# A mixture-of-experts stage: the overflow of the fullest expert computed beside its own block instead of in a 33rd block

## The chip, the cores and the metric

The kernel runs on one core of a Trainium2 chip. The metric is the device time of one execution in microseconds. A profiled execution shows each engine: PE is TensorE, DVE VectorE, ACT ScalarE, POOL GpSimd, SP the queue that issues the loads of weights.

## The reference

Two transformer blocks on 512 tokens of width 1024. The first has a gated linear attention mixer and then the expert layer that this change is about; the second block (retention, a state space mixer, differential attention, two dense feed-forward layers) follows and is not touched. The expert layer is:

```python
logits = (xt @ w_router + b_router)            # 512 tokens, 32 experts
top_vals, top_idx = lax.top_k(logits, 4)
weights = jax.nn.softmax(top_vals, axis=-1)
# per expert e, over its tokens:
gate, up = jnp.split(xblk @ w_gu[e] + b_gu[e], 2, axis=-1)
gate = jnp.minimum(gate, 7.0); up = jnp.clip(up, -7.0, 7.0)
act = (up + 1.0) * gate * jax.nn.sigmoid(1.702 * gate)
y[token] += weight * (act @ w_down[e] + b_down[e])
```

There are 2048 pairs of a token and an expert. Each expert has 3 x 1024 x 1024 weights in fp32, 12.6 MB, and the 32 of them are read once each. For the inputs of this case expert 10 has 131 tokens, expert 17 124, expert 8 121, and expert 0 has 56.

## The kernel before, in words

All engines run one program each, written out in order, and wait for one another by semaphores. The expert stage is `moe_pe`, `moe_act`, `moe_dve` and `moe_pool` (from L2418), with SP in `program_sp`.

Routing (`route_dve`, L2038) ranks the experts by their number of tokens, expert 0 always first. Ranks 0 to 15 take the even positions 0, 2, ... 30 and get wide blocks of 128 rows; ranks 16 to 31 take the odd positions and get narrow blocks of 64 rows. What an expert has beyond its block (`CAP`, 128 or 64) goes to overflow blocks of 128 rows. The first overflow block is block 32, part of the straight program (`N_BLK = 33`); further ones are run by a loop behind the stage (`looped`, L2596) with its own weight loads, whose number of turns is counted on the chip. Block 32 is always run, whether there is an overflow or not.

Each block has 24 weight pieces of 128 x 1024 fp32 (512 KB): 8 of the gate half, 8 of the up half, 8 of the down matrix. The order of the pieces is gate(e), down(e-1), up(e), so phases of 8 wide and of 8 narrow pieces alternate on every engine. SP issues the loads one after another (`fetch`, L438) into 26 slots in turn; a load waits until PE has used the piece that was in the slot.

Wide blocks use every piece three times as fp32r: ACT rounds it (`conv_hi`, L464, out to one of four small buffers), DVE subtracts to get the rest (`conv_lo`, L472, over the raw piece in its slot), and PE makes 6 matmuls of 512 columns (`rows_pe`, L2269): high x high, low x high, high x low, two halves each. Narrow blocks use the raw piece in fp32 (`half_rows_pe`, L2347): the 64 rows are held as weights twice, the two halves of the outputs go to the two halves of the array at once. Each fp32 matmul shows as two instructions in the trace, so a narrow piece has 4.

The rows of a block are gathered by POOL from `hm_scratch`, turned on PE (`turn_pe` for wide, `narrow_xturn_pe` for narrow), multiplied, passed through the gate on ACT and DVE, turned again, multiplied by the down pieces, scaled by the routing weight on ACT and added to `sum_scratch` by a POOL DMA that accumulates (`block_sum`, L2531). Each sum waits for the sum before it. When all sums have landed (`rows_stored`) the loop, if it has turns, and then `combine_sp` (L2698) with the read of `sum_scratch` follow. The first ten pieces of the next layer's weights are loaded on the same SP queue behind the last expert pieces.

The matmul and turn instructions are recorded in helpers: L272 is every matmul, L288 every transpose, L192, L199, L203 and L207 are VectorE operations, L237 ScalarE activations, L451 the loads of SP.

Of the kernel before, what the change touches and what calls it, by code (L numbers as in the profile page):

```python
# [334 lines left out]
def build(nc, ins, out):  # L335
# [35 lines left out]
    s_g = [sem("s_gather0"), sem("s_gather1")]  # L371
    s_y = [sem("s_ystore0"), sem("s_ystore1")]
# [158 lines left out]
    ids, P_FIRST = {}, {}  # L531
    R_MOE = len(W.raws)
# [30 lines left out]
    plan_down(32)  # L563
# [1455 lines left out]
    LH, RH, RP = r(12288, 2048, 128), r(11392, 768, 48), a(4096, 768, 48)  # L2019
# [11 lines left out]
    WSL, ROWF = a(K0 + 208, 48), a(K0 + 304, 48)  # L2031
    ROWI = a(K0 + 256, 48).bitcast(I32)
# [3 lines left out]
    RQ, RTMP = r(5120, 2304, 144), a(K0 + 400, 48)  # L2036

    def route_dve(v):  # L2038
# [35 lines left out]
        v.stt(POS, SMALL, 1.0 - 2.0 * NWIDE, POS, ALU.mult, ALU.add)  # L2074
        v.tt(BASE, CNT, CAP, ALU.subtract)
# [5 lines left out]
        v.stt(BASE, BASE, 32.0, POS, ALU.add, ALU.subtract)  # L2081
# [12 lines left out]
        v.tt(BLK, T1, pos, ALU.add)  # L2094
        OH4 = OH.rearrange("p (t k e) -> p t k e", k=4, e=32)
# [5 lines left out]
        for h in range(2):  # L2101
            is_ = slice(8 * h, 8 * h + 8)
            v.tt(LH[:, is_, :], iota.unsqueeze(1).to_broadcast([128, 8, 128]),
                 OF4[:, is_].unsqueeze(2).to_broadcast([128, 8, 128]), ALU.is_equal)
            v.tt(RP[:, is_, :], iota[:, 0:48].unsqueeze(1).to_broadcast([128, 8, 48]),
                 BK4[:, is_].unsqueeze(2).to_broadcast([128, 8, 48]), ALU.is_equal)
# [17 lines left out]
        v.ts(XI[:, 31:32], XI[:, 31:32], 1.0, 0.0, ALU.subtract, ALU.max)  # L2124
# [13 lines left out]
        v.copy(RQ[:, :, 0:48], RP)  # L2138
        v.tt(RQ[:, :, 48:96], RP, WTH.bitcast(F32).unsqueeze(2).to_broadcast([128, 16, 48]), ALU.mult)
        v.tt(RQ[:, :, 96:144], RP, WTL.unsqueeze(2).to_broadcast([128, 16, 48]), ALU.mult, "slot parts")  # L2140

    def slot_weights_pe(p):

        b = p.bank("slot weights", at=6)
        p.wait_ge(*dve("slot parts"))
        p.claim("slot weights")
        for i in range(16):
            p.mm(PB[b][:, 0:144], LH[:, i, :], RQ[:, i, :], i == 0, i == 15, "slot weights" if i == 15 else None)

    def slot_weights_dve(v):  # L2150

        v.wait_ge(*pe("slot weights"))
        b = bank_of("slot weights")
        v.copy(WSL, b[:, 48:96])
        v.tt(WSL, b[:, 96:144], WSL, ALU.add)
        v.copy(ROWF[:, 0:NBLK], IDXI)
        v.ts(RTMP, b[:, 0:48], SPARE[:, 1:2], SPARE[:, 0:1], ALU.mult, ALU.add)
# [10 lines left out]
    def slot_halves_pe(p):  # L2168

        b = p.bank("slot halves", at=7)  # L2170
        p.wait_ge(*dve("halves"))
        p.claim("slot halves")
        p.mm(PB[b][:, 0:16], TWICE, narrow(WSL), True, True)
        p.mm(PB[b][:, 16:32], TWICE, narrow(ROWF), False, True, "slot halves")

    def slot_halves_dve(v):

        v.wait_ge(*pe("slot halves"))
        b = bank_of("slot halves")
# [11 lines left out]
    def route_pe(p):  # L2191
        rows_out_pe(p, 0)
        b = p.bank("ranks")
        p.wait_ge(*dve("sel"))
        p.claim("ranks")
        sel_ = a(o + 240, 128)
        p.mm(PB[b][:, 0:128], tri, sel_, True, True)
        p.mm(PB[b][:, 128:256], ones, sel_, False, True, "ranks")
        for t in range(1, 4):
            rows_out_pe(p, t)  # L2200
        b = p.bank("slots")
        for i in range(16):
            p.wait_ge(*dve("slots", i // 4))
            if i == 0:
                p.claim("slots")
            p.mm(PB[b][:, 0:48], LH[:, i, :], RH[:, i, :], i == 0, i == 15, "slots" if i == 15 else None)
# [5 lines left out]
    XTs, ATs = a(3072, 512, 64), a(3584, 512, 128)  # L2212
    UT, AC, ZT, GZ = a(6144, 1024), a(7168, 1024), a(8192, 1024), a(9216, 1024)
# [68 lines left out]
    def gu_pe(p, z, e, what, lhs, after=None):  # L2282
        name, b = ("gu", e, what), 2 + 2 * what
        open_pe(p, name, b, lhs, what * 1024)
        p.wait_ge(*z.dve("xg", e))
        for k in range(8):
            rows_pe(p, z, b, XTh[:, k, :], XTl[:, k, :], k, name)
            if after is not None:
                after(k)

    def down_pe(p, z, e, lhs):
        name = ("down", e)
        open_pe(p, name, 6, lhs, 2048)
# [33 lines left out]
    N_BLK = 33  # L2327
# [89 lines left out]

    def moe_pe(p):  # L2418
# [3 lines left out]
        for e in range(N_BLK):  # L2422
            def beside_gate(k):
                if e and k == 2 and is_wide(e):
                    narrow_aturn_pe(p, e - 1)
                if k == 4 and not is_wide(e):
                    aturn_pe(p, MOE, e - 1)
                if e == 0 and k == 2:
                    slot_weights_pe(p)

            def beside_up(k):
                if k == 3 and is_wide(e) and e + 1 < N_BLK:
                    narrow_xturn_pe(p, e + 1)
                if k == 3 and not is_wide(e):
# [13 lines left out]
        aturn_pe(p, MOE, N_BLK - 1)  # L2448
        down_pe(p, MOE, N_BLK - 1, sel(N_BLK - 1))
# [8 lines left out]
    def moe_act(q):  # L2458
        xturn_act(q, MOE, 0)
        for e in range(N_BLK):  # L2460
            if is_wide(e):
# [3 lines left out]
                gate_act(q, MOE, e)  # L2465
                four_units(q, conv_hi)
# [3 lines left out]
                if e + 1 < N_BLK:  # L2470
                    turned_copy_act(q, "xg", e + 1, 0, XTs)
            else:
                halves_act(q, MOE, ("at", e - 1), ATh)
                four_units(q, conv_hi)
# [5 lines left out]
                xturn_act(q, MOE, e + 1)  # L2480
                four_units(q, conv_hi)
        halves_act(q, MOE, ("at", N_BLK - 1), ATh)
        four_units(q, conv_hi)
        four_units(q, conv_hi)
        store_wide(q, N_BLK - 1)

    def moe_dve(v):
        xturn_dve(v, MOE, 0)
        for e in range(N_BLK):
            if is_wide(e):  # L2490
# [3 lines left out]
                gate_dve(v, MOE, e)  # L2494
                four_units(v, conv_lo)
# [3 lines left out]
                up_dve(v, MOE, e)  # L2499
            else:  # L2500
# [20 lines left out]
    def gather_narrow(g, idx, s_):  # L2521
        g.e.indirect_dma_start(out=XG[1][0:64, :], out_offset=None, in_=hm_d,
                               in_offset=bass.IndirectOffsetOnAxis(ap=idx, axis=0)).then_inc(s_, 16)

    def sum_narrow(g, idx, s_):

        g.e.indirect_dma_start(out=sum_d.rearrange("t (h c) -> (t h) c", h=2),
                               out_offset=bass.IndirectOffsetOnAxis(ap=idx, axis=0), in_=YB[1][:, 0:512],
                               in_offset=None, compute_op=ALU.add).then_inc(s_, 16)

    def block_sum(g, e):  # L2531
        g.wait_ge(*act("rows", e))
        if e:
            g.wait_ge(s_y[(e - 1) % 2], 16 * ((e - 1) // 2 + 1))
        if is_wide(e):
            sum_rows(g, 0, ROWI[:, e:e + 1], s_y[0])
        else:
            sum_narrow(g, ROWI[:, e:e + 1], s_y[1])

    def moe_pool(g):  # L2540
# [5 lines left out]
        for e in range(N_BLK):  # L2546
# [4 lines left out]
            else:  # L2551
                gather_narrow(g, IDXI[0:64, e:e + 1], s_g[1])
# [43 lines left out]
    def looped(q, name, body):  # L2596
# [6 lines left out]
        n_ = q.e.value_load(SI[0:1, 16:17], min_val=0, max_val=15)  # L2603
# [6 lines left out]
    def loop_sp(s):  # L2610
        def body(x):
            if at_pe.known:
                which[0] = x.e.value_load(SI[0:1, bass.ds(x.loop[0] + 1, 1)], min_val=0, max_val=31)
# [16 lines left out]
    def loop_dve(v):  # L2630
        def body(x):
            x.copy(WJ, WSL[:, bass.ds(x.loop[0] + 33, 1)])
            x.copy(SELJ[0:96, :], SELX[0:96, bass.ds(x.loop[0] + 1, 1)].to_broadcast([96, 128]), "sel")
# [1439 lines left out]
    def program_sp(s):  # L4073
        load_sp(s)
        for i in range(len(W.pieces)):
            if P_FIRST.get(i, 0) and at_pe.known:
                e = P_FIRST[i]
                s.wait_ge(*dve("ids"))
                ids[e] = s.e.value_load(SIP[0:1, e:e + 1] if e < 32 else SI[0:1, 0:1], min_val=0, max_val=31)
# [77 lines left out]
```

## Time and profile before

| what | value |
|---|---|
| median of 3 runs | 3135.3 us (3132.92 to 3135.72) |
| the profiled execution: time, span | 3138.64 us, 3136.4 us |
| PE busy over the span | 2866.5 us (91%) |
| DVE, ACT, POOL busy | 1645.6 us (52%), 1201.9 us (38%), 269.5 us (9%) |
| DMA moved | 634.58 MB, mean 202 GB/s |
| expert stage | from about 456 to about 1580 us of the span |

The span is what lies between the first and the last instruction of the trace; the time adds 2.2 us around it. All stretches below are microseconds from the span's start. A busy PE is not PE at its peak, and a share is an average over stages with different limits, so the rows further down are from inside the expert stage.

### The profile page before, as it was taken

The page shows a single profiled execution, that of the slowest core. Times are in us where ns is not written, and L with a number is a line of the kernel's source. Part 1 is how long each engine was busy: PE and PEld are TensorE (multiplying, and loading weights), DVE is VectorE, ACT ScalarE, POOL GpSimd, SP SyncE. Part 2 cuts the span into 40 slices and gives each one's busy share as a digit, 9 for nine tenths or more (in the row PEclk, how much of TensorE's full clock was granted, in tenths as well). Part 3 has the DMA queues.
Part 4 walks back from the last instruction along what each step waited for, and adds up shares of the span by engine and source line. Part 5 has one row for each costly group of instructions (what it writes and reads, how often), then busy time and mean ns, then how long its engine had stood idle before and what let it go on. Part 6 is the DMA issues. An engine that isn't in the chain of part 4 may idle for free.

```text
span 3136.4 us, 35266 instructions
## 1 busy us (share of the span) xinstructions
PE 2866.5 (91%) x13014; PEld 2047.2 (65%) x13014; DVE 1645.6 (52%) x2034; ACT 1201.9 (38%) x1549; POOL 269.5 (9%) x233
## 2 busy tenths in 40 slices
PE   6988879999999999999979778999998988999998
PEld 3856656655455555555567567888886755888887
DVE  5557556655555545555654535344356556543445
ACT  3242325544444544444532114322243256332334
POOL 1054721010010010000000000000000000000000
PEclk8998969999999999999979879999999988999999
DMA  7244739999999999999943022233332210223210
GB/s 223 73 137 166 269 140 383 397 391 396 397 392 394 396 394 393 395 393 392 368 159 95 13 108 74 91 98 98 97 101 74 81 35 20 89 90 106 88 61 27
DMA packets 224021, 634.58 MB, mean 202 GB/s; under 512 B 20038, under 2 KB 38484, under 8 KB 222980
## 3 DMA queue, kind: packets, MB, share of 16 engines
q1 hardware_dynamic: 207984, 577.70, 50.0%
q0 software_dynamic: 11760, 42.99, 4.9%
q10 hardware_dynamic: 4100, 11.59, 1.0%
q8 instruction: 104, 1.70, 0.2%
q14 instruction: 73, 0.60, 0.1%
HBM read 603.89 MB, written 28.31 MB: 202 GB/s over the span
## 4 chain that ended last, share of the span: by engine, by line
PE 63%; DMA 15%; DVE 9%; SPq 7%; ACT 3%; issue 2%; DVEq 0%; ACTq 0%; POOLq 0%
PE ps L272 61%; SPq L451 7%; DMA ring<-in_w_gu 7%; DMA arena<-in_w_gu 4%; DMA ring<-in_w_down 3%; DVE arena L192 2%; PE ps L288 2%; ACT arena L237 1%; ACT wunits L464 1%; DVE ring_r L472 1%; DVE arena L203 1%; DVE arena L211 1%; DVE arena L215 1%; DMA arena<-in_ctx 1%; DVE arena_r L203 1%
## 5 line engine op out<-in xcount | busy, mean ns | idle before, releaser
L272 PE MATMUL ps<-arena_r,wunits 128*128 128x512 f32 (+1 forms) x3552 | 1112.8, 395 | 15.6 <-DVE arena_r L192 7.8
L472 DVE TENSOR_TENSOR ring_r<-ring,wunits 128x1024 fp32r<-128x1024 f32 (+1 forms) x533 | 638.4, 1217 | 716.8 <-ACT wunits L464 709.8
L464 ACT ACTIVATE wunits<-ring 128x1024 fp32r<-128x1024 f32 (+1 forms) x533 | 552.4, 1050 | 835.6 <-PE ps L272 647.7
L272 PEld LDWEIGHTS ps<-arena_r,wunits 128*128 128x128 f32 x3552 | 672.1, 191 | 165.3 <-issue 15.8
L272 PE MATMUL ps<-arena_r,ring_r 128*128 128x512 f32 (+1 forms) x1776 | 696.0, 392 | 0.0
L272 PE MATMUL ps<-wunits,arena_r 128*128 128x512 f32 x1984 | 570.1, 401 | 57.5 <-ACT wunits L464 47.4
L272 PEld LDWEIGHTS ps<-wunits,arena_r 128*128 128x128 f32 x1984 | 369.0, 190 | 163.9 <-ACT wunits L464 35.7
L272 PEld LDWEIGHTS ps<-arena_r,ring_r 128*128 128x128 f32 x1776 | 338.0, 190 | 70.7
L272 PE MATMUL ps<-arena 128*64 128x512 f32 (+10 forms) x1566 | 307.8, 438 | 50.2 <-DVE arena L207 16.1
L272 PEld LDWEIGHTS ps<-arena 128*64 128x64 f32 (+5 forms) x1566 | 168.5, 181 | 172.4 <-issue 84.1
L272 PE MATMUL ps<-ring,arena 128*64 128x512 f32 (+1 forms) x1080 | 261.0, 601 | 10.2 <-issue 5.7
L272 PE MATMUL ps<-ring_r,arena_r 128*128 128x512 f32 x756 | 256.1, 401 | 8.6 <-DVE ring_r L472 5.0
L237 ACT ACTIVATE arena<-ps 128x512 f32<-128x512 f32 (+4 forms) x222 | 133.8, 603 | 210.2 <-PE ps L272 156.3
L272 PEld LDWEIGHTS ps<-ring_r,arena_r 128*128 128x128 f32 x756 | 139.7, 190 | 58.8 <-DVE ring_r L472 30.0
L272 PEld LDWEIGHTS ps<-ring,arena 128*64 128x64 f32 (+1 forms) x1080 | 75.8, 139 | 153.1 <-issue 108.2
L472 DVE TENSOR_TENSOR arena_r<-arena,wunits 128x1024 fp32r<-128x1024 f32 x118 | 141.6, 1223 | 51.3 <-ACT wunits L464 48.9
L288 PE MATMUL ps<-KC,arena 128*128 128x128 f32 (+3 forms) x742 | 110.1, 291 | 49.9 <-DVE arena L203 15.9
L464 ACT ACTIVATE wunits<-arena 128x1024 fp32r<-128x1024 f32 x118 | 123.5, 1058 | 76.8 <-DMA arena<-in_w_gu 59.3
L192 DVE TENSOR_TENSOR arena_r<-ps,arena_r 128x1024 fp32r<-128x1024 f32 (+1 forms) x38 | 44.4, 1169 | 200.7 <-ACT arena_r L237 200.2
L288 PEld LDWEIGHTS ps<-KC,arena 128*128 128x128 f32 (+3 forms) x742 | 86.5, 154 | 92.4 <-issue 49.4
L237 ACT ACTIVATE arena<-arena 128x512 f32<-128x512 f32 (+5 forms) x140 | 73.8, 527 | 139.4 <-DVE arena L192 85.2
L237 ACT ACTIVATE arena_r<-ps 128x1024 fp32r<-128x1024 f32 (+2 forms) x39 | 37.8, 970 | 232.6 <-PE ps L288 232.2
(176 smaller groups left out, 1970.8 us busy)
## 6 DMA issues: line engine op xcount, KB each, us to landing
ring<-in_w_gu SPq DMA_DIRECT2D x382, 512.0 KB, 15.9
ring<-in_w_down SPq DMA_DIRECT2D x170, 512.0 KB, 16.9
arena<-in_w_gu SPq DMA_DIRECT2D x146, 512.0 KB, 15.9
arena<-in_w_down SPq DMA_DIRECT2D x94, 512.0 KB, 16.4
ring<-in_w_ada SPq DMA_DIRECT2D x48, 512.0 KB, 5.4
ring<-in_ffn_w_gate SPq DMA_DIRECT2D x44, 512.0 KB, 3.7
ring<-in_ffn_w_up SPq DMA_DIRECT2D x44, 512.0 KB, 3.7
ring<-in_ffn_w_down SPq DMA_DIRECT2D x40, 512.0 KB, 3.6
```

The source lines that it names most:

```text
L192: self.inc(self.e.tensor_tensor(o, x, y, op), key)
L203: self.inc(self.e.scalar_tensor_tensor(out=o, in0=x, scalar=s, in1=y, op0=op0, op1=op1), key)
L211: self.inc(self.e.reciprocal(o, x), key)
L215: self.inc(self.e.tensor_reduce(o, x, AX.X, op), key)
L237: self.inc(self.e.activation(o, x, f, **kw), key)
L272: ins = self.e.matmul(o, l_, r_, start=start, stop=stop, skip_group_check=True)
L288: ins = self.e.transpose(o, x, self.ident[0:k, 0:k])
L451: s.e.dma_start(dst, w.src()).then_inc(w.sem, 16)
L464: q.inc(q.e.activation(h, raw, ACT.Copy), (st.tag, "hi", i))
L472: q.inc(q.e.tensor_tensor(lo, raw, h.bitcast(F32), ALU.subtract), (st.tag, "lo", i))
```

## The change

Block 32 is taken out (`N_BLK = 32`), with its 24 pieces, its gather and its sum. Position 20 (`TWIN`) now belongs to the fullest expert beside expert 0 (rank 1), which changes places with rank 10, and its cap is 192 rows: 128 in the wide block 20 and up to 64 in a twin block. The twin is computed in fp32 in two halves of the array, like a narrow block, from the raw pieces of block 20 while they lie in their slots. PE's order at block 20 is two twin pieces ahead, then one twin piece and one wide piece in turn, in all three phases (gate, up, down). DVE's `conv_lo` of these 24 pieces waits until PE has read the raw piece. The twin has a gather of its own (issued behind that of block 12), a turn beside block 19, gate, up and row scaling behind those of block 20 (the down phase of both lies in block 21), and a sum of its own behind the sum of block 20.

The stage now ends with block 31, a narrow one: its last phase is 8 narrow down pieces. Tables of 48 columns have 50. The loop behind the stage now starts at overflow block 0 instead of 1 and has no turn where nothing is left over. Its core:

```diff
-    for e_ in range(33):
+    for e_ in range(32):
...
+        v.ts(BASE, RANK, 1.0, 64.0, ALU.is_equal, ALU.mult)
+        v.tt(CAP, CAP, BASE, ALU.add)
+        v.stt(POS, BASE, (TWIN - 2) / 64.0, POS, ALU.mult, ALU.add)
+        v.ts(BASE, RANK, TWIN / 2.0, 2.0 - TWIN, ALU.is_equal, ALU.mult)
+        v.tt(POS, POS, BASE, ALU.add)
...
+        v.ts(T1f, OFf, 127.5, None, ALU.is_gt, None)
+        v.stt(OFf, T1f, -128.0, OFf, ALU.mult, ALU.add)
+        v.stt(BKf, T1f, 32.0 - TWIN, BKf, ALU.mult, ALU.add)
...
     def conv_lo(q, st, i):
...
+            if st.tag == "w" and U_TWIN <= i < U_TWIN + 24:
+                q.wait_ge(*pe("twin read", i))
...
     def gu_pe(p, z, e, what, lhs, after=None):
...
+        if e == TWIN:
+            open_halves_pe(p, ("twin", what), 7, twin_sel(), what * 1024)
+            p.wait_ge(*act("twin xt"))
+            for k in range(2):
+                twin_rows_pe(p, 7, TWX[:, k, :], what, k)
         p.wait_ge(*z.dve("xg", e))
         for k in range(8):
+            if e == TWIN and k + 2 < 8:
+                twin_rows_pe(p, 7, TWX[:, k + 2, :], what, k + 2)
             rows_pe(p, z, b, XTh[:, k, :], XTl[:, k, :], k, name)
...
     def down_pe(p, z, e, lhs):
...
+        if e == TWIN:
+            open_halves_pe(p, ("twin", 2), 5, twin_sel(), 2048)
+            p.wait_ge(*act("twin at"))
...
+    def twin_rows_pe(p, b, lhs, part, k):
+
+        i = U_TWIN + 8 * part + k
+        u = W.units[i]
+        land(p, u.w)
+        _, raw, _ = unit_tiles(u)
+        for h, o_, cs in each_half(b):
+            p.mm(o_, lhs, raw[:, cs], False, k == 7, ("twin", part) if k == 7 and h else None, h == 1)
+        p.note(("twin read", i))
...
+    def twin_gate_act(q):
+        q.wait_ge(*pe("twin", 0))
+        q.act(TWZ, PB[7], ACT.Sigmoid, "twin gate", scale=1.702)
...
+    def twin_up_dve(v):
+        v.wait_ge(*pe("twin", 1))
+        v.ts(UT[:, 0:512], PB[7], -6.0, 8.0, ALU.max, ALU.min)
+        v.free(("twin", 1))
+        v.stt(TWA, TWG, TOP, UT[:, 0:512], ALU.min, ALU.mult, "twin acts")
...
     def moe_pe(p):
...
+                if k == 1 and e == TWIN - 1:
+                    twin_xturn_pe(p)
...
+                if k == 7 and e == TWIN + 1:
+                    twin_aturn_pe(p)
...
-        aturn_pe(p, MOE, N_BLK - 1)
-        down_pe(p, MOE, N_BLK - 1, sel(N_BLK - 1))
+        narrow_aturn_pe(p, N_BLK - 1)
+        narrow_down_pe(p, N_BLK - 1)
...
     def block_sum(g, e):
...
+        if e == TWIN:
+            g.wait_ge(*act("twin rows"))
+            g.wait_ge(s_y[0], 16 * (e // 2 + 1))
+            sum_narrow(g, TWY, ROWI[:, 32:33], s_yt)
```

## Rows read from the trace of the kernel before

**Rows 1.** The page: busy tenths of the DMA engines in 40 slices.
```profile
DMA  7244739999999999999943022233332210223210
```

**Rows 2.** Windows: stretch, length, busy time of each engine, clock, DMA share, GB/s.
```profile
471.00:491.00 20.00, 18.14 (x89) 11.83 (x89) 13.36 (x14) 9.18 (x10) 2.92 (x1) 1.00 0.98 359
...
740.51:1424.58 684.07, 634.48 (x2802) 358.18 (x2802) 369.50 (x320) 316.85 (x320) 58.60 (x40) 0.99 1.03 394
```

**Rows 3.** The chain of waits, expert stage: start, length, what.
```profile
570.51 1.04 PE ps L288 x8
...
631.61 1.04 PE ps L288 x8
...
740.51 1.02 PE ps L288 x8
...
1424.58 1.02 PE ps L288 x8
```

**Rows 4.** Timeline, routing and the stage's start: start, length, engine, line.
```profile
420.02 0.19 DVE L203 SCALAR_TENSOR_TENSOR arena<-arena 128x32 f32<-128x32 f32 x1
...
426.06 0.62 DVE L203 SCALAR_TENSOR_TENSOR arena<-arena 128x128 f32<-128x128 f32 x2
...
446.34 1.60 SPq L451 DMA_DIRECT2D ring<-in_w_gu  x2
...
455.78 2.08 PE L272 MATMUL ps<-wunits,arena_r 128*128 128x512 f32 x4 [7.45 <-DVE arena_r L192]
```

**Rows 5.** DMA queues and issues, 1000 to 1400 us: share; us to landing.
```profile
q1 hardware_dynamic: 40512, 147.51, 93.3%
q0 software_dynamic: 3072, 9.44, 9.3%
...
ring<-in_w_gu SPq DMA_DIRECT2D x122, 512.0 KB, 16.4
```

**Rows 6.** Timeline of PE, a narrow phase and part of a wide one.
```profile
1030.77 0.41 PE L272 MATMUL ps<-BPT,arena 96*64 96x512 bf16 x2
1031.01 3.60 PE L272 MATMUL ps<-ring,arena 128*64 128x512 f32 x16
1034.54 1.09 PE L288 MATMUL ps<-KC,arena 128*128 128x128 f32 x8
1035.56 3.65 PE L272 MATMUL ps<-ring,arena 128*64 128x512 f32 x16
...
1051.92 1.07 PE L272 MATMUL ps<-wunits,arena_r 128*128 128x512 f32 x4
...
1053.28 1.07 PE L272 MATMUL ps<-wunits,arena_r 128*128 128x512 f32 x4
```

**Rows 7.** Waits of SP's queue, 470 to 680 us: total, times, longest.
```profile
SPq L451 <- PE ps L272: 53.7, 67, 3.7
```

**Rows 8.** The page, costliest groups: busy and mean ns, idle before.
```profile
L472 DVE TENSOR_TENSOR ring_r<-ring,wunits 128x1024 fp32r<-128x1024 f32 (+1 forms) x533 | 638.4, 1217 | 716.8 <-ACT wunits L464 709.8
```

**Rows 9.** DMA issues, 1544.5 to 1545.5 us: us from issue to landing.
```profile
ring<-in_w_down SPq DMA_DIRECT2D x1, 512.0 KB, 16.7
```

**Rows 10.** The chain of waits at the stage's end.
```profile
1545.42 8.76 DMA sum_scratch<-arena
...
1573.22 5.96 DMA sum_scratch<-arena
```

**Rows 11.** Timeline at the stage's end, SP and PE.
```profile
1543.72 0.93 SPq L451 DMA_DIRECT2D ring<-in_w_down  x1
...
1584.98 3.68 PE L288 MATMUL ps<-KC,ring 128*128 128x128 f32 x16 [13.37 <-DMA ring<-sum_scratch]
```

**Rows 12.** Windows at the stage's end, columns as in rows 2.
```profile
1556.00:1560.00 4.00, 2.48 (x7) 1.31 (x6) 2.54 (x3) 3.59 (x4) 0.00 (x0) 0.50 0.72 252
```

**Rows 13.** The page: issues of w_gu, KB each, us to landing.
```profile
ring<-in_w_gu SPq DMA_DIRECT2D x382, 512.0 KB, 15.9
...
arena<-in_w_gu SPq DMA_DIRECT2D x146, 512.0 KB, 15.9
```

More of the change, by code:

```diff
@@ L531, in build @@
     ids, P_FIRST = {}, {}
+    U_TWIN = len(W.units) + 12 * TWIN
     R_MOE = len(W.raws)
@@ L2137, in route_dve @@
             v.wait_ge(s_, 32)
-        v.copy(RQ[:, :, 0:48], RP)
-        v.tt(RQ[:, :, 48:96], RP, WTH.bitcast(F32).unsqueeze(2).to_broadcast([128, 16, 48]), ALU.mult)
-        v.tt(RQ[:, :, 96:144], RP, WTL.unsqueeze(2).to_broadcast([128, 16, 48]), ALU.mult, "slot parts")
+        v.copy(RQ[:, :, 0:NBLK], RP)
+        v.tt(RQ[:, :, NBLK:2 * NBLK], RP, WTH.bitcast(F32).unsqueeze(2).to_broadcast([128, 16, NBLK]), ALU.mult)
+        v.tt(RQ[:, :, 2 * NBLK:3 * NBLK], RP, WTL.unsqueeze(2).to_broadcast([128, 16, NBLK]), ALU.mult, "slot parts")
     def slot_weights_pe(p):
@@ L2147, in slot_weights_pe @@
         for i in range(16):
-            p.mm(PB[b][:, 0:144], LH[:, i, :], RQ[:, i, :], i == 0, i == 15, "slot weights" if i == 15 else None)
+            p.mm(PB[b][:, 0:3 * NBLK], LH[:, i, :], RQ[:, i, :], i == 0, i == 15, "slot weights" if i == 15 else None)
     def slot_weights_dve(v):
@@ L2173, in slot_halves_pe @@
         p.mm(PB[b][:, 0:16], TWICE, narrow(WSL), True, True)
-        p.mm(PB[b][:, 16:32], TWICE, narrow(ROWF), False, True, "slot halves")
+        p.mm(PB[b][:, 16:32], TWICE, narrow(ROWF), False, True)
+        p.mm(PB[b][:, 32:33], TWICE, WSL[:, 32:33], False, True)
+        p.mm(PB[b][:, 33:34], TWICE, ROWF[:, 32:33], False, True, "slot halves")
     def slot_halves_dve(v):
@@ L2205, in route_pe @@
                 p.claim("slots")
-            p.mm(PB[b][:, 0:48], LH[:, i, :], RH[:, i, :], i == 0, i == 15, "slots" if i == 15 else None)
+            p.mm(PB[b][:, 0:NBLK], LH[:, i, :], RH[:, i, :], i == 0, i == 15, "slots" if i == 15 else None)
     XG = [a(0, 1024), a(1024, 1024)]
@@ L2293, in down_pe, with twin @@
         open_pe(p, name, 6, lhs, 2048)
+        def twin(k):
+            twin_rows_pe(p, 5, TWT[:, k % 4, k // 4 * 64:k // 4 * 64 + 64], 2, k)
+        if e == TWIN:
+            open_halves_pe(p, ("twin", 2), 5, twin_sel(), 2048)
+            p.wait_ge(*act("twin at"))
+            for k in range(2):
+                twin(k)
         p.wait_ge(*z.dve("at", e))
         for k in range(8):
+            if e == TWIN and k + 2 < 8:
+                twin(k + 2)
             rows_pe(p, z, 6, ATh[:, k, :], ATl[:, k, :], k, name)
@@ L2416, in narrow_rows_act, with twin_sel, twin_xturn_pe, twin_aturn_pe @@
         q.free(("down", e))
+    def twin_sel():
+        return SELB[0:96, TWIN:TWIN + 1].to_broadcast([96, 64])
+    def twin_xturn_pe(p):
+        name = ("twin xt",)
+        p.wait_ge(s_gt, 16)
+        p.bank(name, at=0)
+        p.claim(name)
+        for k in range(8):
+            p.tp(PB[0][:, k * 64:(k + 1) * 64], TWR[:, k * 128:(k + 1) * 128], name if k == 7 else None)
+    def twin_aturn_pe(p):
+        name = ("twin at",)
+        p.wait_ge(*dve("twin acts"))
+        p.bank(name, at=0)
+        p.claim(name)
+        for c in range(4):
+            p.tp(PB[0][:, c * 128:(c + 1) * 128], TWA[:, c * 128:(c + 1) * 128], name if c == 3 else None)
+    def twin_copy_act(q, name, o_):
+        q.wait_ge(*pe(name))
+        q.copy(flat(o_), PB[0], name)
+        q.free((name,))
+    def twin_rows_pe(p, b, lhs, part, k):
[9 more added lines that the diff above has]
+        q.act(TWZ, PB[7], ACT.Sigmoid, "twin gate", scale=1.702)
+    def twin_gate_dve(v):
+        v.wait_ge(*act("twin gate"))
+        v.stt(TWG, PB[7], 7.0, TWZ, ALU.min, ALU.mult)
+        v.free(("twin", 0))
+    def twin_up_dve(v):
[3 more added lines that the diff above has]
+        v.stt(TWA, TWG, TOP, UT[:, 0:512], ALU.min, ALU.mult, "twin acts")
+    def twin_rows_act(q):
+        q.wait_ge(*pe("twin", 2))
+        q.act(TWY, PB[5], ACT.Copy, "twin rows", scale=WSL[:, 32:33])
+        q.free(("twin", 2))
     def moe_pe(p):
@@ L2433, in beside_up @@
                     narrow_xturn_pe(p, e + 1)
-                if k == 3 and not is_wide(e):
+                if k == 3 and not is_wide(e) and e + 1 < N_BLK:
                     xturn_pe(p, MOE, e + 1, 0, gathered(e + 1))
@@ L2612, in body @@
             if at_pe.known:
-                which[0] = x.e.value_load(SI[0:1, bass.ds(x.loop[0] + 1, 1)], min_val=0, max_val=31)
+                which[0] = x.e.value_load(SI[0:1, bass.ds(x.loop[0], 1)], min_val=0, max_val=31)
             for i in range(len(LW.pieces)):
@@ L2632, in body @@
             x.copy(WJ, WSL[:, bass.ds(x.loop[0] + 33, 1)])
-            x.copy(SELJ[0:96, :], SELX[0:96, bass.ds(x.loop[0] + 1, 1)].to_broadcast([96, 128]), "sel")
+            x.copy(SELJ[0:96, :], SELX[0:96, bass.ds(x.loop[0], 1)].to_broadcast([96, 128]), "sel")
             for i in range(NUNIT):
@@ L4078, in program_sp @@
                 s.wait_ge(*dve("ids"))
-                ids[e] = s.e.value_load(SIP[0:1, e:e + 1] if e < 32 else SI[0:1, 0:1], min_val=0, max_val=31)
+                ids[e] = s.e.value_load(SIP[0:1, e:e + 1], min_val=0, max_val=31)
             fetch(s, W, i)
```

86 lines of the change are left out of this document (52 added, 34 removed).

## The prediction

> **What bounds the kernel now.** I read the page first, for where the span is dense, then the chain of waits from 380 to 1600 us, then windows, waits and the timeline inside that stretch, which is the expert stage. The slices of the page say that the DMA engines are full from slice 6 to slice 19 and nowhere else for long [rows 1]; there the reader is to see a stage of 1.1 ms that moves weights all the time. The windows give the stretch from 740.51 to 1424.58 us its numbers: DMA share 1.03, PE busy 634.48 of 684.07 us, clock 0.99 [rows 2]. Both are nearly full, so the question is which of them sets the pace. The chain answers it. The 8 transposes of a wide block start 61.1 us apart in the first part (570.51 to 631.61, full clock) and 68.4 us apart later ((1424.58 - 740.51) / 10) [rows 3]. A pair of blocks (one wide, one narrow) thus costs PE 61.1 us when it never waits, and 68.4 us when it waits for weights: PE starts at 455.78 us with full slots [rows 4], is late, catches up 7.3 us a pair, and from about 680 us on it is paced by landings.
>
> DMA's pair of 68.4 us has two parts. The hardware queue that carries the weights has 93.3 of 102.6 parts, the software queue of the gathers and sums 9.3 [rows 5]. So 48 weight pieces take 62.2 us, **1.296 us a piece**, and 6.2 us go to the gather and the sum of both blocks. A wide block gathers and adds twice the bytes of a narrow one (128 rows of 4 KB against 64), so these are 6 units of **1.03 us**.
>
> **What goes.** Block 32 is a wide one: 24 pieces x 1.296 = 31.1 us of transfers and one wide gather, 2.1 us. Its sum stood behind the last weights; in the new order the sum of block 31 stands there, and the twin's sum takes its place among the weights, so the count of sums before the last landing is unchanged. For the last landing: -33.2 us.
>
> **What the twin adds on the DMA side.** No weights (it multiplies the pieces of block 20 in place), one narrow gather: +1.0 us.
>
> **What the twin adds on PE.** A narrow piece is 4 fp32 instructions; 16 of them (4 pieces) take from 1031.01 to 1034.54, so 0.88 us a piece [rows 6]. 24 x 0.88 = 21.1. Three openings of two halves, 0.24 each (1030.77 to 1031.01) = 0.7. Eight transposes of the rows, at most the 1.02 of eight full ones (1034.54 to 1035.56), and four of the activations, 0.5: 1.5. Then the alternation, which no row shows: a piece of the twin now stands between wide rows, so the array goes from full width to two halves and back, 7 groups in each of 3 phases, 42 changes. Below: nothing (narrow phases run on into transposes in 3.53 us, 8 slots of 0.43 would be 3.44). Above: a whole wide matmul each, (1053.28 - 1051.92) / 6 = 0.227 us [rows 6], 9.5 us. I take 0.12, nearest to the 0.09 left over in the 3.53: 5 us. Sum 28 us, between 23 and 33.
>
> The Trainium skill speaks against such an alternation: TensorEngine Tiling (Array Packing), section Key Properties, says that a change of tiling mode drains the engine. With the warm constant of 0.166 us of TensorE: Matmul & The Clock Gate, section Single matmul latency, 42 drains would be an estimate of 7 us instead of 5; no row here shows such a drain in isolation.
>
> **Does PE's extra work reach the end?** Blocks 20 and 21 cost PE 61.1 + 28 = 89 us against 69.4 on the DMA side: PE is 20 us late after them, and 3 us more at its worst, since a last narrow phase gains that much back. Two rows say what a late PE does to DMA. In the steady part a piece lands 16.4 us after its issue [rows 5], that is 11.5 of the 26 slots at 68.4 / 48 = 1.425 us; the other 14.5 slots are 20.6 us of room before SP has to wait for a slot, and then 16.4 us of queue are to be emptied before an engine idles. The views agree: between 680 and 1500 us SP's waits have no entry at all, between 470 and 680, where PE is late by some 3.5 pairs x 7.3 = 26 us at first, SP waits 53.7 us in 67 pieces [rows 7], and the DMA share still is 0.98 there [rows 2]. So a lag of 23 us has been seen and cost DMA at most 5% of some 20 us: **+1.0 us**, bounds 0 and 8. It is worked off at 7.3 us a pair in 2.8 pairs; 5 pairs are left.
>
> The added waits: VectorE may write the low part over a raw piece only after the twin has read it. PE reads two pieces ahead; after the first twin piece it still has two twin pieces (1.76) and four wide matmuls (0.9) to do before it needs that low part, and the subtraction takes 1.22 us [rows 8]: covered. ScalarE's copy of the twin's turned activations holds back its conversions of the down pieces by some 3 us; PE fills this with two twin pieces, and what stays is lag, in the bounds above. The POOL queue waits for the landing of block 20's sum before it issues the twin's; behind it stands the gather for block 24, needed a pair later.
>
> **Routing.** Before the block ids exist VectorE gets 5 operations of 32 columns (0.19 + 0.02 us) and 3 of 128 columns (two take 0.62, so 0.31) [rows 4], and slightly wider compares, 0.1. SP issues the pieces of block 1 at 446.34, right behind the ids [rows 4], with DMA not yet full. So this is on the path: 1.05 + 0.93 + 0.1 = **+2.1 us** (bounds 1 and 4, as the gather chain runs beside it).
>
> **The end of the stage.** The last weight piece of before is issued at 1543.72 and takes 16.7 us [rows 9, 11]: landed at 1560.4. Behind it stand most of a wide phase on PE, the scaling and the sum, which is issued at 1573.22 and lands 5.96 later, 1579.18 [rows 10]: 18.8 us behind the last landing. PE resumes at 1584.98 [rows 11], another 5.8 us later. After: the last eight pieces are narrow. Their activations are ready before they land (8 x 1.3 = 10.4 us ahead, minus 0.9 for the last up piece and about 3 for clamp, product, turn and copy), so PE follows the landings and ends 1 us after the last. But PE idles there a few us, and in such a gap the granted clock went to 0.50 (1.2 GHz) in the same place of before [rows 12]; 8 pieces at half rate take 14 us instead of 7, of which I count 2 us. Scaling 0.7, issue 0.4, and the sum 8.8, as the narrow one issued at 1545.42 beside busy queues took 8.76 [rows 10] (5.96 is the lower bound). 1 + 2 + 0.7 + 0.4 + 8.8 = 12.9 against 18.8: **-5.9 us**, bounds -10 and 0. The ten pieces of the next layer are issued earlier and still land when the sums are read back: +1.0 (0 to 3).
>
> **Sum.** -31.1 - 2.1 + 1.0 + 1.0 + 2.1 - 5.9 + 1.0 = -34.0 us. What follows is PE at work without a wait for transfers, so it moves with it. The profiled execution took 3138.6 us (span 3136.4), the sum gives 3104.6 for it; it stands 3.3 above the median of the runs, 3135.3, which gives **3101.3 us**.
>
> **Rivals.** (1) The lag of PE reaches DMA. For it: the stage has only 7.3 us of PE slack a pair, the 28 us is one lump, and the changes of width are priced by no row. Against: the start of the stage [rows 2, 7]. If nothing of the lag were absorbed the 20 us come back: 3121 us; a part of it, 3113 to 3121. Chance 0.10. (2) The end gives more: the sum lands in 6 us, no half clock, free queues: 4 us below, and routing beside other work, 1: 3096. It is inside the range, chance 0.12. (3) Slower than before: the loop behind the blocks runs. It decides from one expert on that overflows its cap. Now one overflow has a block, and the page shows 528 pieces of w_gu, 33 x 16, so no turn was run [rows 13]; after it must be the fullest expert beside expert 0 and hold at most 192. A turn has nothing beside it: gather and sum at 8.8 each, two turns with their splits at about 3.3, three wide phases at 8 x 1.36 + 0.6, activations and scaling about 4, 63 us: 3164. Against it: the routing worked out from the inputs gives 131 rows to expert 10, 124 to the next, 56 to expert 0, and 61 to the seventeenth in the order, which is the first with 64 places. Chance 0.03.
>
> **How the numbers follow.** The forecast case has 0.75: 3101. The bounds of its terms, added as if independent, are about 9 us to either side; down to 3090 holds rival 2, up to 3114 takes in the milder half of rival 1. A change under 0.2% (6 us) is what a measurement of this kernel can't tell from none: faster by more 0.94, since even a whole unabsorbed lag leaves 14 us; within 0.02; slower 0.04.
>
> **What would show it.** Right: the transposes of wide blocks still 68.4 us apart away from block 20; DMA share 1.03 through it; no PE wait for landings in about the three pairs behind it; 512 pieces of w_gu instead of 528; the sum of the last block some 13 us behind the last landing; the next layer's first transposes 34 us earlier. Wrong: a DMA share clearly under 1 around block 20 (rival 1), twin pieces that take over 1.2 us of PE each, a second set of loads from the loop (rival 3), or a stage end as long behind the last landing as now.

## The result, and the profile after

The changed kernel takes **3103.2 us** (median of 4 runs, 3100.6 to 3106.8), the kernel before on the same chip 3135.5 (3132.9 to 3137.1). The ratio is **0.9891**, 95% interval 0.9879 to 0.9903, so 32.3 us less by the medians; the ratio's interval is 30 to 38 us. The profiled execution took 3106.83 us, its span 3104.7.

The page has one block of weights less: 370 + 142 = 512 pieces of w_gu where there were 528 [rows 13]. The slices of the DMA engines are full through the stage as before [rows 1]. The twin shows only in the bytes: 347 GB/s in the slice from 1164 to 1242 us, where its neighbours have 400 and 392.

```profile
DMA  7244829999999999999943022233332210323210
GB/s 225 71 133 165 282 95 379 390 396 390 392 396 396 390 400 347 392 389 396 388 149 95 4 107 87 89 102 99 99 96 74 82 29 24 93 88 102 94 56 28
ring<-in_w_gu SPq DMA_DIRECT2D x370, 512.0 KB, 15.7
arena<-in_w_gu SPq DMA_DIRECT2D x142, 512.0 KB, 15.8
```

**One mark for all traces.** What lies ahead of the routing varies by some us from one execution to the next: the routing's first reduction stands at 416.47 us in the profiled execution before, at 418.53 in the one after, and between 414.7 and 423.9 in the others. So I count from that reduction to the first transposes of the sums read back (1584.98 in [rows 11], 1555.02 after). That is 1168.5 us before and 1136.5 after, **32.0 us less**; the rest of the kernel behind it is 1.7 us shorter.

**Routing and start.** The timeline after, VectorE, SP and PE (start, length, engine, line):

```profile
418.53 1.03 DVE L216 TENSOR_REDUCE arena<-arena 128x128 f32<-128x512 f32 x1
...
450.48 1.77 SPq L453 DMA_DIRECT2D ring<-in_w_gu  x2
...
459.81 1.65 PE L273 MATMUL ps<-wunits,arena_r 128*128 128x512 f32 x3 [7.38 <-DVE arena_r L193]
```

From the mark to PE's start it is 41.28 us; before it was 455.78 [rows 4] - 416.47 = 39.31. So +1.97, where +2.1 was forecast. The first 50 us behind that start, from 4 us after it, are a little less dense. Windows of before, then of after (stretch, length, busy time of PE, PEld, DVE, ACT, POOL, clock, DMA share, GB/s):

```profile
460.00:510.00 50.00, 48.14 (x233) 32.66 (x233) 30.90 (x36) 24.48 (x25) 4.55 (x2) 1.00 1.01 390
```

```profile
464.00:514.00 50.00, 48.16 (x224) 33.73 (x224) 31.58 (x38) 24.54 (x25) 1.10 (x2) 0.95 0.99 371
```

The share is 1.01 and 0.99, so by the share some 1.0 us of transfers (0.02 x 50) are lost here. The bytes say more (371 GB/s against 390), and so do the landings, where a trace has them for every piece: counted from the mark, the 220th of SP's expert pieces lands at 331.9 us before and at 335.8 after. Of these 3.9 us 2.0 are the routing and **1.9 the start of the stage**. PE is as busy in both (48.1 us), but at a mean clock of 0.95 instead of 1.00 and with 224 matmuls instead of 233.

**The twin on PE.** The timeline of PE in the twin's first phase. A 128*64 group is a twin piece, the 128*128 groups of 4 and 2 are a wide one:

```profile
1132.54 1.08 PE L273 MATMUL ps<-ring,arena 128*64 128x512 f32 x4
1133.55 1.20 PE L273 MATMUL ps<-wunits,arena_r 128*128 128x512 f32 x4
1134.59 0.62 PE L273 MATMUL ps<-ring_r,arena_r 128*128 128x512 f32 x2
1135.14 1.08 PE L273 MATMUL ps<-ring,arena 128*64 128x512 f32 x4
```

One turn, 1132.54 to 1135.14, is 2.60 us. Alone, a wide piece is 1.36 ([rows 6]: 1051.92 to 1053.28) and a narrow one 0.88, together 2.24. The two changes of width thus cost 0.36 us, 0.18 each.

Behind the twin the transposes of wide blocks tell who sets the pace:

```profile
1205.19 1.09 PE L289 MATMUL ps<-KC,arena 128*128 128x128 f32 x8
...
1266.29 1.09 PE L289 MATMUL ps<-KC,arena 128*128 128x128 f32 x8
...
1327.39 1.09 PE L289 MATMUL ps<-KC,arena 128*128 128x128 f32 x8
```

61.1 us apart, the number that [rows 3] show where PE never waits, not the 68.4 of a stage paced by landings: PE works its lag off. The same transposes of block 20 start at 1111.43, so the pair with the twin took 93.8 us.

**Did the lag reach DMA?** Windows after, and the waits of SP's queue from 680 to 1500 us, which had no entry there before:

```profile
1120.00:1130.00 10.00, 9.23 (x28) 3.69 (x24) 3.68 (x3) 4.18 (x5) 0.00 (x0) 0.66 1.03 412
...
1180.00:1190.00 10.00, 10.00 (x45) 4.56 (x44) 5.92 (x6) 7.09 (x8) 0.00 (x0) 1.00 0.96 372
1190.00:1200.00 10.00, 10.00 (x42) 5.53 (x41) 4.40 (x4) 2.11 (x2) 0.00 (x0) 1.00 0.72 254
1200.00:1210.00 10.00, 10.00 (x50) 4.10 (x49) 1.31 (x2) 5.48 (x6) 1.57 (x1) 1.00 0.92 269
1210.00:1220.00 10.00, 8.79 (x41) 6.95 (x40) 9.97 (x10) 5.98 (x7) 2.97 (x2) 1.00 1.02 349
```

```profile
SPq L453 <- PE ps L273: 50.3, 51, 5.2
```

It did. Against a full share of 1.03 the three windows from 1180 to 1210 lack 0.07 + 0.31 + 0.11, together 0.49 x 10 us, or 4.8 us of transfers at the full share. I use this sum below as **the hole** of a run.

**The end of the stage.** PE's last narrow piece, SP's loads for the next layer and PE's return from the timeline, and the last sum from the chain of waits:

```profile
1521.50 20.47 SPq L453 DMA_DIRECT2D ring<-in_ret_s_w_in  x10
...
1538.78 1.08 PE L273 MATMUL ps<-ring,arena 128*64 128x512 f32 x4 [0.21 <-DMA ring<-in_w_down]
...
1555.02 4.07 PE L289 MATMUL ps<-KC,ring 128*128 128x128 f32 x16 [15.16 <-DMA ring<-sum_scratch]
```

```profile
1541.05 7.66 DMA sum_scratch<-arena
```

The last piece starts as it lands, 1538.78; the sum is issued 2.3 us later and has landed at 1548.71, 9.9 us behind the last landing instead of 18.8 [rows 9 to 11]. PE returns 6.3 us after that (5.8 before).

**The account.** From the mark to the last landing: 1560.4 - 416.47 = 1143.9 before, 1538.78 - 418.53 = 1120.3 after, -23.7. Last landing to sum landed: -8.9. Sum landed to PE: +0.5. Together -32.1; the transposes' -32.0 is the same within rounding.

### The profile page after: what moved, and what is told of

The parts are those of the page before. It is cut to its first block, busy times and chain, and to the rows that moved or that the text cites. A ratio compares the mean times of both kernels' runs of the same rounds, so it can differ in the third digit from the quotient of the medians.

```text
span 3104.7 us, 35015 instructions
## 1 busy us (share of the span) xinstructions
PE 2844.3 (92%) x12966; PEld 2025.7 (65%) x12966; DVE 1611.8 (52%) x2017; ACT 1171.7 (38%) x1525; POOL 265.1 (9%) x233
## 4 chain that ended last, share of the span: by engine, by line
PE 68%; DMA 10%; DVE 9%; SPq 7%; ACT 3%; issue 2%; DVEq 0%; ACTq 0%; POOLq 0%
PE ps L273 66%; SPq L453 6%; DMA ring<-in_w_gu 5%; DVE arena L193 2%; PE ps L289 2%; DMA ring<-in_w_down 2%; ACT wunits L466 1%; DMA arena<-in_w_gu 1%; DMA arena<-in_w_down 1%; ACT arena L238 1%; DVE arena L204 1%; DVE ring_r L476 1%; DVE arena L212 1%; DVE arena_r L204 1%; DVE arena L216 1%
## 5 line engine op out<-in xcount | busy, mean ns | idle before, releaser
L476 DVE TENSOR_TENSOR ring_r<-ring,wunits 128x1024 fp32r<-128x1024 f32 (+1 forms) x513 | 612.5, 1216 | 720.7 <-ACT wunits L466 691.1
L466 ACT ACTIVATE wunits<-ring 128x1024 fp32r<-128x1024 f32 (+1 forms) x513 | 529.9, 1049 | 817.7 <-PE ps L273 672.0
L273 PE MATMUL ps<-wunits,arena_r 128*128 128x512 f32 x1888 | 544.8, 402 | 39.9 <-ACT wunits L466 32.4
L273 PEld LDWEIGHTS ps<-wunits,arena_r 128*128 128x128 f32 x1888 | 351.4, 190 | 148.7 <-issue 30.9
L273 PE MATMUL ps<-arena 128*64 128x512 f32 (+11 forms) x1578 | 308.7, 438 | 48.8 <-DVE arena L208 14.7
L273 PE MATMUL ps<-ring,arena 128*64 128x512 f32 (+1 forms) x1168 | 283.7, 604 | 13.3 <-issue 5.7
L273 PE MATMUL ps<-ring_r,arena_r 128*128 128x512 f32 x716 | 242.6, 400 | 9.1 <-DVE ring_r L476 6.4
L238 ACT ACTIVATE arena<-ps 128x512 f32<-128x512 f32 (+5 forms) x224 | 134.5, 600 | 231.7 <-PE ps L273 161.7
L273 PEld LDWEIGHTS ps<-ring_r,arena_r 128*128 128x128 f32 x716 | 133.3, 190 | 53.0 <-DVE ring_r L476 24.7
L193 POOL TENSOR_TENSOR ring<-ring 128x512 f32<-128x512 f32 (+5 forms) x90 | 107.7, 1196 | 189.4 <-DVE ring L193 137.9
```

The costliest lines, as they stand in the source:

```text
L193: self.inc(self.e.tensor_tensor(o, x, y, op), key)
L238: self.inc(self.e.activation(o, x, f, **kw), key)
L273: ins = self.e.matmul(o, l_, r_, start=start, stop=stop, skip_group_check=True)
L466: q.inc(q.e.activation(h, raw, ACT.Copy), (st.tag, "hi", i))
```

## The experiments

Two theories were on trial. **Theory A**: the twin costs about 28 us of PE time in one lump; the slots of weights ahead absorb most of it, the rest is a hole in the transfers, and the pairs behind work the lag off at 7.3 us each. **Theory B**: the gain is the 24 pieces less, and the twin itself, wherever it stands, costs nothing that can be seen. The short numbers behind each run: time, ratio to the kernel before on the same chip with its interval, and, from the profile, mark to transposes (1136.5 in the run above).

**No twin.** All its work on PE, VectorE, ScalarE and POOL is left out, and with it the rows of expert 10 beyond 128.

```
-            if e == TWIN and k + 2 < 8:
-                twin_rows_pe(p, 7, TWX[:, k + 2, :], what, k + 2)
...
-            if e == TWIN - 8:
-                gather_narrow(g, TWR, IDXI[0:64, 32:33], s_gt)
```

> The changed kernel without the twin's work: no gather, turns, matmuls, activations, sum or waits of the twin; routing and all else stay. It leaves out the rows of the overflow (three of one expert). Theory (the lag of PE in blocks 20 and 21 empties the DMA queue for some 5 us, and the twin's gather and sum take 2 us of DMA time): some 7 us below the changed kernel, 3096 us, and no stretch between 480 and 1510 us with a DMA share under 1.0. Rival (the lag is absorbed whole, only the twin's own transfers cost): 2 us below, 3101 us.

Measured: 3095.6 us, 0.9871 (0.9855 to 0.9888), 1132.2 us. The same window as the hole's middle, and SP's waits from 680 to 1500 us:

```profile
1190.00:1200.00 10.00, 9.95 (x48) 7.11 (x50) 6.99 (x6) 5.88 (x6) 0.00 (x0) 1.00 1.03 409
```

```profile
SPq L453 <- PE ps L273: 0.4, 1, 0.4
```

Without the twin there is no hole. By the marks the twin costs 4.3 us (3.3 against the changed kernel's second run, further down), by the ratios 6.3 (0.0020 x 3135.5), and neither is clear of what else varies. The landings of single pieces are, counted from the mark: the 220th of SP's expert pieces lands at 337.4 us here and at 335.8 in the changed kernel, so this run lost 1.6 us more before the twin had done anything; the last lands at 1115.1 and 1120.2. The twin thus costs 1.6 + 5.1 = **6.7 us** of transfers. Its own gather and sum are 2 units of 1.03 [rows 5], the hole is 4.8: 6.9 together. The time went as A had it; B's 3101 is above all four times (3095.1 to 3098.5), though only at the edge of the ratio's interval.

**The twin later, at block 28.** Two pairs are left behind it instead of five.

```
-TWIN = 20
+TWIN = 28
```

> The twin at position 28 instead of 20, nothing else. Theory (PE works its lag of some 18 us off at 7.3 us a pair, and here one pair is left): PE ends 11 us behind the landings instead of 1, so about 9 us above the changed kernel, 3112 us. Rival (the place does not matter, the lag costs only what it costs at block 20): 3103 us.

Measured: 3111.3 us, 0.9931 (0.9914 to 0.9948), 1145.1 us: 8.6 more than at block 20. Windows around the twin, and the last sum from the chain:

```profile
1460.00:1470.00 10.00, 10.00 (x42) 5.54 (x41) 4.20 (x4) 2.11 (x2) 0.00 (x0) 1.00 0.79 277
1470.00:1480.00 10.00, 10.00 (x51) 4.10 (x49) 1.51 (x2) 5.68 (x7) 1.57 (x1) 1.00 0.88 269
```

```profile
1550.74 4.76 DMA sum_scratch<-arena
```

The hole is the usual size (4.2 us). What is new is that PE still is late when the last weights have landed (at 1533.4): from 1530 to 1540 PE is busy for 9.59 of 10 us at a DMA share of 0.69. The sum is issued at 1550.74, 9.7 us later than after, and only then does the stage end. Part comes back, as that sum meets an emptier queue (4.76 us instead of 7.66).

**The twin earlier, at block 4.** There PE still has the lag of the stage's start. The twin's rows are gathered one block ahead of it, not eight.

```
-TWIN = 20
+TWIN = 4
-            if e == TWIN - 8:
+            if e == TWIN - 1:
```

> The twin at position 4, its gather behind that of block 3. Theory (PE is still some 11 us late from the start of the stage, and the slots have no more room for it): the DMA queue runs empty for some 16 us instead of 5, 3114 us, DMA share clearly under 1 between about 590 and 680 us. Rival (DMA loses the same few us wherever the twin lies): 3103 us.

Measured: 3113.3 us, 0.9927 (0.9911 to 0.9944), 1144.1 us. The windows behind the twin:

```profile
640.00:650.00 10.00, 10.00 (x45) 4.26 (x42) 5.65 (x7) 7.10 (x8) 0.00 (x0) 1.00 0.92 351
650.00:660.00 10.00, 10.00 (x41) 5.53 (x40) 4.79 (x4) 2.11 (x2) 0.00 (x0) 1.00 0.62 209
660.00:680.00 20.00, 18.82 (x90) 11.05 (x89) 10.89 (x11) 11.45 (x12) 5.01 (x3) 1.00 0.93 308
```

The hole is (1.1 + 4.1 + 2.0) / 1.03 = 7.0 us, and SP waits 105.9 us between 470 and 680, where it is 66.9 with the twin at block 20 (53.7 before [rows 7]). Two lags add up, and less of them is absorbed. The later gather isn't the cause: between 560 and 680 us PE waits once, 1.2 us, and for VectorE. With both ends worse than the middle, B has fallen: the place is worth 8.6 and 7.6 us by the marks, 8.1 and 10.1 by the medians, 12.5 and 11.3 by the ratios.

**The same twin with fewer changes of width.** The pieces of two of the three phases are worked in one group at the start of the phase, those of the gate phase in a group of four and two pairs. In the changed kernel the first three pieces of a phase stand together and five stand alone, so it has 6 groups a phase, 18 in all; here 5 are left (the expectation below counts 21), that is 13 fewer, with two changes of width each. The work is the same. It was run twice, the second time with the changed kernel again beside it.

```
-            for k in range(2):
-                twin_rows_pe(p, 7, TWX[:, k, :], what, k)
+            for k in range(8 if what else 2):
+                twin_rows_pe(p, 7, TWX[:, k, :], what, k)
...
-            for k in range(2):
+            for k in range(8):
                 twin(k)
```

> The twin at position 20, but in the gate phase its pieces go in groups of two, and in the up and down phases all eight go ahead of the wide pieces: 5 groups instead of 21 between full-width matmuls. Theory (each change between full width and two halves costs PE 0.17 us, since a step with a twin piece takes 2.59 us against 1.36 + 0.88): PE is 5 to 6 us less late, the DMA queue hardly empties, 3 to 5 us below the changed kernel, 3099 us. Rival (the 0.35 us a group are no changes but longer fp32 pieces, or the late release of the slots by eight pieces costs the same): no gain, 3103 us.

Measured: 3105.1 us, 0.9898 (0.9881 to 0.9914), 1133.6 us. The expected 3099 did not come, though the trace did what it should. Its mark stands at 423.94 us: 5 to 9 us later than elsewhere, before anything that was changed. So it was run once more, beside the changed kernel.

> The changed kernel again, unchanged, as the yardstick of this set: 3103 us by its own runs so far.

> The kernel with the twin's pieces ahead of the wide ones again, beside the changed kernel on one chip. Its trace was 3.9 us shorter from the routing's first reduction to the landing of the last sum (1126.3 against 1130.2), while its median was not lower. Theory (those 3.9 us are real, and the medians of the first set differ by where the executions stood before the routing): 3 to 4 us below the changed kernel of this set. Rival (nothing is won): equal within 1 us.

Measured: the changed kernel 3105.0 us, 0.9891 (0.9876 to 0.9906), 1135.5 us; the grouped twin 3102.0 us, 0.9889 (0.9873 to 0.9906), 1134.1 us. The times can't tell the two apart: the medians differ by 3.0 us, the ratios by 0.6. The traces can: windows of the changed kernel's second run, then of the grouped twin, then SP's waits of the latter from 680 to 1500 us.

```profile
1180.00:1190.00 10.00, 10.00 (x40) 4.71 (x39) 6.06 (x6) 5.24 (x6) 0.00 (x0) 1.00 0.98 381
1190.00:1200.00 10.00, 10.00 (x46) 5.70 (x46) 2.45 (x2) 2.13 (x3) 1.47 (x1) 1.00 0.83 284
1200.00:1210.00 10.00, 8.79 (x44) 4.35 (x39) 5.67 (x6) 5.85 (x6) 0.10 (x1) 1.00 1.01 290
```

```profile
1180.00:1190.00 10.00, 10.00 (x45) 7.31 (x42) 5.93 (x6) 4.25 (x4) 0.00 (x0) 1.00 0.99 383
1190.00:1200.00 10.00, 10.00 (x51) 4.83 (x51) 1.22 (x1) 4.25 (x5) 1.57 (x1) 1.00 1.00 374
```

```profile
SPq L453 <- PE ps L273: 23.8, 26, 4.3
```

The pair with the twin takes 91.0 us in the changed kernel here (transposes at 1109.77 and 1200.80) and 86.6 in the grouped one (1109.79 and 1196.42): 4.4 us for 13 groups fewer, 0.34 each, 0.17 a change. The hole shrinks from 2.6 to 0.7 us, and mark to transposes by 1.4. The mechanism is as A has it, and its worth in time is 1 to 3 us and not 4: at least a part of what is saved on PE had been hidden.

This pair of runs also bears on why two executions of the *same* kernel have holes of 4.8 and 2.6 us. PE waits 1.81 us for a landing just ahead of the twin in both. Windows of the execution above, then of this one:

```profile
1120.00:1124.00 4.00, 3.23 (x9) 0.82 (x6) 1.66 (x2) 2.80 (x3) 0.00 (x0) 0.60 1.02 418
1124.00:1128.00 4.00, 4.00 (x11) 1.70 (x9) 0.79 (x1) 1.06 (x1) 0.00 (x0) 0.55 1.03 408
```

```profile
1120.00:1124.00 4.00, 4.00 (x16) 1.77 (x14) 1.99 (x3) 2.90 (x3) 0.00 (x0) 1.00 1.03 416
1124.00:1128.00 4.00, 4.00 (x19) 2.31 (x17) 2.08 (x2) 1.21 (x2) 0.00 (x0) 1.00 1.03 410
```

In the one the granted clock fell to its lower level (0.60 and 0.55 are means of a stretch with parts at 1.2 and parts at 2.4 GHz), in the other it stayed at 2.4. The pair took 93.8 us there and 91.0 here, so the dip goes with 2.7 us more lag, and the hole is 2.2 us larger. The grouped twin had the dip in its first run (0.57 from 1126 to 1130) and not in its second: there the pair took 87.8 and 86.6 us, and the holes are 0.8 and 0.7. So a dip goes with a longer pair both times; that it makes the hole larger is not shown.

**Fewer loads of the next layer ahead of the read.** The grouped twin, and SP issues 4 instead of 10 pieces of the next layer before it reads the sums back.

```
-        for i in range(10):
+        for i in range(4):
             fetch(s, X, i)
         rows_stored(s)
...
-        for i in range(10, len(X.pieces)):
+        for i in range(4, len(X.pieces)):
```

> The same, and only 4 instead of 10 pieces of the next layer are loaded ahead of the read of the sums; the other 6 come behind it. Theory (the last sum lands after 7.5 us instead of 6.0 and the first tile of the read after 5.2 to 6.1 instead of 4.7 because those pieces fill the DMA engines): another 2 to 3 us less. Rival (the next layer then waits for its pieces): no gain, or slower by up to 3 us.

Measured: 3100.9 us (3095.7 to 3102.7), 0.9881 (0.9866 to 0.9896), 1130.2 us. SP and PE from the timeline, the sum from the chain:

```profile
1515.58 8.75 SPq L453 DMA_DIRECT2D ring<-in_ret_s_w_in  x4
...
1544.98 3.68 PE L289 MATMUL ps<-KC,ring 128*128 128x128 f32 x16 [11.77 <-DMA ring<-sum_scratch]
```

```profile
1534.40 4.69 DMA sum_scratch<-arena
```

The sum lands in 4.69 us instead of 7.66 (7.48 and 7.18 in the two runs beside it), and from its issue to PE's return it is 10.6 us instead of 14.0 (14.8 in the two runs beside it). By the marks that is 3.8 us; in the medians it is 1.1, with overlapping intervals. It is the fastest version that computes everything, and that it beats the changed kernel is shown by the traces alone.

**Fewer slots.** 22 slots of weights instead of 26, in the changed kernel and in the kernel before. By A a twin with less room behind it should cost the changed kernel more than the kernel before.

```
-            W.slots = PARK[4:] + PARK[0:4] + MORE + [x for x in W.slots if x not in PARK]
+            W.slots = PARK[4:] + PARK[0:4] + MORE[:4] + [x for x in W.slots if x not in PARK]
```

> The changed kernel with 22 weight slots instead of 26 in the expert stage. Theory (the slots are what takes up PE's lag): 4 pieces less are loaded ahead at the stage's start, 4 x 1.3 = 5 us, and at block 20 the queue runs empty for 4 x 1.4 = 6 us more, together 11 us above the changed kernel, 3114 us. Rival (slots matter for the start alone): 5 us above, 3108 us.

> The kernel before with 22 weight slots instead of 26. It has no twin and so no such lag after its start. Both theories: 4 pieces less are loaded ahead, 5 us above the kernel before, 3141 us; what the 22 slots cost the changed kernel beyond this is the twin's.

Measured: the changed kernel 3113.6 us, 0.9920 (0.9906 to 0.9933), 1145.7 us; the kernel before 3142.2 us, 1.0018 (1.0008 to 1.0027), 1174.7 us. So four slots are worth 8.6 us of the median to the one (9.1 by the ratios) and 6.6 to the other (5.6); by the marks 9.7 (the mean of its two runs taken) and 6.2. The start of the stage in the kernel before, with 26 slots and with 22, both from 20 to 100 us behind the mark; then the middle of the hole in the changed kernel with 22:

```profile
436.47:516.47 80.00, 62.55 (x284) 41.77 (x284) 51.16 (x70) 31.37 (x32) 9.89 (x6) 0.85 0.85 314
```

```profile
439.18:519.18 80.00, 62.62 (x284) 41.84 (x284) 51.08 (x70) 31.36 (x32) 9.79 (x6) 0.85 0.83 283
```

```profile
1190.00:1200.00 10.00, 10.00 (x41) 5.46 (x40) 4.91 (x4) 2.48 (x3) 0.00 (x0) 1.00 0.65 215
```

Both kernels pay at the start of the stage, where PE's first lag meets fewer slots. The kernel before moves 31 GB/s less over these 80 us, 2.5 MB or 4.7 pieces, 6.1 us at 1.296 a piece: this is the whole of its 6.2. The landings agree: its 220th piece lands 5.5 us later than with 26 slots (337.4 against 331.9 from the mark), its last 5.6. The share, 0.85 and 0.83, shows a small part of it. In the changed kernel the same stretch falls from 296 to 269 GB/s, 5.3 us. The twin's part is the difference of the two kernels, 3.5 us by the marks and the ratios and 2.0 by the medians; by the times alone it is not clear of noise, but the hole from 1160 to 1210 grows to 6.7 us (from 4.8 and 2.6). Direction and place are A's. Its size, 6 us for four slots at 1.425 us a piece, is too large. A likely reason, argued and not shown, is that a missing slot costs only when the queue runs dry.

## Why the prediction was right, step by step

- **The time.** 3101.3 forecast, 3103.2 measured, inside 3090 to 3114. By the marks -34.0 was forecast and -32.0 came. That the total fits so well is in part luck: the last landing came 5.4 us less early than the steps gave, and the way from there to PE's return 3.5 us shorter.
- **Fewer pieces, gathers, routing** (-31.1, -2.1, +1.0, +2.1). The routing is measured apart: +1.97. The run without the twin tests the others together. There the last piece starts, as it lands, at 1531.76, 1115.1 us behind the mark; that is 28.8 us less than the 1143.9 of before. The terms without the twin, -31.1 - 2.1 - 1.0 (a sum less) + 2.1, make -32.1. The 3.3 us between are the start of the stage, which the sum put at nothing: at the 220th piece this run is 5.5 us behind the kernel before (337.4 against 331.9), 2.0 of it by the routing, so 3.5 by the start. Why the start loses more here than in the changed kernel (1.9) stays open. The pieces themselves were sized well: in the trace of before the last 24 land within 32.6 us (1111.4 to 1144.0 from the mark).
- **The twin on PE, 28 us (23 to 33).** The pair took 91.0 us in the undisturbed execution, of which 2.6 were waits for landings ahead of the twin: 91.0 - 2.6 - 61.1 = **27.3**. The term was right; one part in it was small. A change of width costs 0.17 to 0.18 us and not 0.12, and there are 36 and not 42 of them, as the forecast counted 7 groups a phase where the trace has 6: 6.1 to 6.5 us instead of 5. Here the Trainium skill was nearer than my row: TensorEngine Tiling (Array Packing), section Key Properties, says that a change of tiling mode drains the engine, and the 0.166 us of TensorE: Matmul & The Clock Gate, section Single matmul latency, agrees with 0.17 to 0.18. The runs don't separate the change of tiling from the change between fp32r and fp32 that comes with it. I had 0.12 from the ends of narrow phases that run on into transposes; those show one change at most.
- **The lag reaches DMA: +1.0 taken, 0 to 8 allowed.** This term was mis-sized: the hole is 4.8 us in the profiled execution, 2.6 in the second one. The last landing came 23.7 us earlier; the steps gave -33.2 + 1.0 + 1.0 + 2.1 = -29.1. Of the 5.4 us between, 3.8 are the hole beyond the 1.0, and 1.9 the start of the stage, for which the sum had no term; the other steps erred by 0.3 the other way. I had taken the size from a place where PE was late by 26 us and DMA at 0.98 [rows 2, 7]. A likely reason, argued and not shown, is that there the lag only shrinks; around the twin it grows from nothing while transfers run at full rate, and is highest when all slots are taken. The rival that the whole lag comes through (3113 to 3121) did not happen, a part of it did.
- **Absorbed by slots, worked off at 7.3 us a pair.** Shown: transposes 61.1 us apart behind the twin. At block 28 the lag isn't worked off in time and shows at the end, at block 4 it meets another one.
- **The end of the stage: -5.9 taken, -10 to 0 allowed.** -8.9 came. The 2 us for a half clock did not: the granted clock was 1.00 from 1516 to 1540, and the last narrow pieces ran as they landed, most of them 1.28 us apart. The sum took 7.66 and not 8.8. The last piece took 1.1, scaling and issue 1.2, as counted. Reading back cost +0.5 of the +1.0.
- **The other rivals.** The loop behind the blocks did not run (512 pieces, none more). "The end gives more" was half right: more did come there, and the hole took it back.

## What to carry to other kernels

Where a stage is paced by transfers and the compute engine has a few us of slack a turn, a lump of extra compute is nearly free when three things hold: the buffers ahead hold about its length, the turns behind it have slack enough to work it off, and no other lag stands next to it. Put it in the middle, and look for the hole in the transfers towards its end (here the twin ran from 1117 to 1200 us, the hole from 1180 to 1210). Price the hole apart: a place where an old lag dies away showed less of it than the twin made.

Before a difference of 1 to 3 us is read from two profiles, fix a mark behind whatever varies from one execution to the next and count from there, and count landed pieces or bytes beside the busy share: the start with 22 slots lost 6 us of transfers while the share fell from 0.85 to 0.83.

## What the runs showed of the hardware

- A change between full-width fp32r matmuls and two halves in fp32 costs 0.17 to 0.18 us (from 13 groups less, and from one turn of 2.60 us).
- A wait of 1.8 us of PE in front of the twin was followed by a granted clock of 0.55 to 0.60 over 8 us in one execution and of 1.00 in another of the same kernel. The first took 2.7 us longer for the pair. With the grouped twin the two outcomes lie 1.2 us apart.
- An accumulating store of 64 rows took 7.18 to 7.66 us with ten loads of 512 KB queued beside it (the changed kernel and the grouped twin) and 4.69 with four.
- The part ahead of the routing varied between 414.7 and 423.9 us over the profiled executions, for code that no experiment touched. Runs that were not profiled have no mark, so how much of the spread of the times it makes is not shown; it is wide enough to hide a gain of 1.4 us.
